# Gated delta rule in a diffusion trunk kernel: beta folded into the block inverses, 64-column products in place of masked 128-column ones, element work redistributed over four engines, and a final norm by tiles

## The chip, the cores and the metric

One core of a Trainium2 chip runs the whole program as one launch. The metric is the device time in microseconds; smaller is better. All arithmetic named here is float32.

## The reference

The reference is one inference step of a two-layer trunk over 1152 tokens (1024 of a sample, 128 of a prompt) with width 1024. Two parts of it matter.

The first is the gated DeltaNet of layer 1, which runs over each sequence forwards and backwards, with 8 heads of 64. For a chunk with keys K, queries Q, values V, gates beta and summed log-decays gc, let gamma[i,j] = exp(gc[i] - gc[j]) for j <= i. It solves A U = beta V and A W = beta exp(gc) K, with A = I + strict(beta K K^T gamma); then, with a state S that goes from chunk to chunk,

```python
v_new = u_i - w_i @ S
o = (q * exp(gc)) @ S + (tril(q @ k.T) * gamma) @ v_new
S = S * exp(g_last) + (k * exp(g_last - gc)).T @ v_new
```

The second is the final RMSNorm: y = x * rsqrt(mean(x*x) + eps) * gain, for each token.

## The kernel before

The program is a row of stages with a barrier between any two. The stages of the delta rule are `delta_prepare` (gdnp), `delta_blocks` (gdna), `delta_chunks` (gdnc) and `delta_outputs` (gdno); `final_norm` comes last.

The kernel uses chunks of 128 tokens: 9 tiles, 2 directions, 18 items (`items`). `delta_blocks` writes K K^T and Q K^T of each tile to DRAM and inverts the 16 x 16 diagonal blocks of A on VectorE; its M is first scaled by beta, with one instruction for each half of the partitions (L2243).

`delta_chunks` handles three items at a time in a software pipeline: iteration n prepares item n+1, inverts item n and carries the state through item n-1. The inverse T is built from its 16-blocks in three levels (32, 64, 128). A level computes, for each head, W = part^T T, then T W, and subtracts it. `part` is the decayed K K^T masked by GpSimd to the blocks that this level joins (L2537, `joins`); beta is a factor with which ScalarE takes W out of PSUM (L2415). Levels 1 and 2 also transpose T on TensorE (L2384), and ScalarE copies that to TT (L2419). VectorE subtracts (L2513, and on TT in the last level L2515). A level's products are written in two groups of four heads, `hg`, with one PSUM bank each for a and b.

The state part (`scan`) has four steps: step 0 multiplies K and Q by S (L2347) and VectorE forms r = beta V - beta exp(gc) K S (L2465, L2469) and mq (L2466); step 1 is T r (L2354), copied to vn (L2474); step 2 is AT vn (L2359), added up in mq and o (L2481, L2486, L2488); step 3 is kd^T vn (L2363), by which VectorE updates S in eight instructions (L2495). Steps 1 and 2 take 128 columns for a head, of which 64 are used.

The preparation: E is the row of gc broadcast to all partitions by a DMA (L2313); VectorE subtracts (L2433), ScalarE takes abs (L2423) and exp (L2428), which gives `gam`. VectorE multiplies kg (L2444) and AT (L2457) by gam, writes T's blocks by the mask `own` (L2447) and makes egk and egl, 8 numbers a partition (L2452, L2454). GpSimd masks AT (L2541), makes the three parts, TT's blocks (L2549), vb = beta V (L2555) and kd (L2562).

Every engine's order is written out by hand and kept by semaphores; TensorE interleaves level li's first products, scan step li, then level li's second products. SyncE issues each item's loads in order and waits before each for its buffer. In `final_norm` SyncE loads 9 tiles of x and then the gain. ScalarE squares and sums each tile and takes a root for groups of 4, 4 and 1 tiles (L235, L239). VectorE scales all tiles of a group (L253), multiplies each by the gain (L1925), and SyncE stores it (L1910).

## Time and profile before

| | us |
|---|---|
| median of 3 runs (lowest, highest) | 4721.29 (4719.97, 4725.55) |
| the profiled execution's own time | 4717.61 |
| its span | 4715.8 |
| delta_chunks: first load issued to the state's last update | 3112.0 to 3591.1 |
| final_norm: first load issued to the end of the span | 4680.1 to 4715.8 |

Times in the rows are microseconds from the start of the span, "mean" is in ns. A float32 product shows as two records of PE (and two weight loads, PEld), a transpose as one. L lines are those of the kernel before. "xN" counts the records merged into a row; in brackets stand the idle time ahead of it and what ended it.

### The profile page before, as it was taken

To read this page: it belongs to the slowest core of one execution; us is meant where nothing else is said; L and a number is where in the kernel's file an instruction comes from. 1 tells how busy PE (TensorE), PEld (TensorE's weight loads), DVE (VectorE), ACT (ScalarE), POOL (GpSimd) and SP (SyncE) were. 2 spreads that over 40 slices of the span, in tenths; PEclk is the share of its full clock that TensorE was granted. 3 is DMA by queue.
4 is the path that set the end of the run, shared out by engine and by line. 5 is a ranking of instruction groups with operands and counts; after the bars stand their busy time and mean duration, and the time that the engine had idled before them with its cause. 6 is when DMAs were issued, how large, how long until landed. Compare 5 with 4: busy or idle time off the path is not lost. (4 is left out here: it accounts for less than half of the span.)

```text
span 4715.8 us, 62439 instructions
## 1 busy us (share of the span) xinstructions
PE 3943.4 (84%) x25842; PEld 3420.0 (73%) x25842; DVE 1757.2 (37%) x3337; ACT 866.7 (18%) x2008; POOL 683.1 (14%) x521
## 2 busy tenths in 40 slices
PE   4979978986769999996999597438886859999995
PEld 3976623444569999995999475338885659999995
DVE  3245541224531211123123454677876441121112
ACT  2113320001100110012111123424443100011001
POOL 2000110111100011002000000036651101001100
PEclk7988979997889999997999798768997979999998
DMA  4226412314547777773421402332223547777774
GB/s 151 89 82 233 148 67 98 137 40 149 201 148 268 261 266 264 268 257 117 116 89 67 108 8 76 102 88 60 73 65 130 190 154 264 268 259 267 266 268 155
DMA packets 353335, 744.94 MB, mean 158 GB/s; under 512 B 87432, under 2 KB 193559, under 8 KB 351976
## 3 DMA queue, kind: packets, MB, share of 16 engines
q1 hardware_dynamic: 333066, 683.15, 40.9%
q0 software_dynamic: 17392, 57.58, 4.5%
q8 instruction: 205, 3.36, 0.3%
q10 hardware_dynamic: 2618, 0.40, 0.1%
q14 instruction: 54, 0.44, 0.0%
HBM read 635.63 MB, written 106.10 MB: 157 GB/s over the span
## 5 line engine op out<-in xcount | busy, mean ns | idle before, releaser
L1826 PE MATMUL moe_b<-moe_xT,ffn_w 128*128 128x144 f32 x8192 | 1022.9, 287 | 0.0
L1826 PEld LDWEIGHTS moe_b<-moe_xT,ffn_w 128*128 128x128 f32 x8192 | 1012.7, 191 | 1.8
L1826 PE MATMUL moe_b<-moe_gu,ffn_w 128*128 128x144 f32 x4096 | 550.7, 288 | 0.0
L1826 PEld LDWEIGHTS moe_b<-moe_gu,ffn_w 128*128 128x128 f32 x4096 | 516.3, 190 | 4.8
L1871 DVE TENSOR_TENSOR moe_gu<-moe_sg,moe_b 128x144 f32<-128x144 f32 x256 | 77.9, 304 | 782.3 <-PE moe_b L1826 782.3
L1851 ACT ACTIVATE moe_yT<-moe_b 128x144 f32<-128x144 f32 x256 | 74.6, 291 | 1074.8 <-PE moe_b L1826 1074.8
L2380 PE MATMUL gdnc_a<-gdnc_T,gdnc_part 128*128 128x128 f32 x864 | 139.3, 318 | 156.7 <-POOL gdnc_part L2537 88.0
L1859 DVE TENSOR_SCALAR moe_xT<-moe_x,keep_coef 128x128 f32<-128x128 f32 (+1 forms) x544 | 154.7, 346 | 252.2 <-PE moe_x L1778 252.1
L2380 PEld LDWEIGHTS gdnc_a<-gdnc_T,gdnc_part 128*128 128x128 f32 x864 | 128.0, 229 | 162.7 <-POOL gdnc_part L2537 149.9
L1747 POOL DMA_INDIRECT scratch_x<-moe_ys,moe_slot x32 | 51.8, 1619 | 1260.7 <-DVE moe_yp L1881 1260.7
L297 PE MATMUL proj_mm<-proj_hT_low,proj_w_high 128*128 128x384 f32 x576 | 193.2, 335 | 0.0
L297 PE MATMUL proj_mm<-proj_hT_high,proj_w_low 128*128 128x384 f32 x576 | 193.1, 335 | 0.0
L297 PE MATMUL proj_mm<-proj_hT_high,proj_w_high 128*128 128x384 f32 x576 | 193.1, 335 | 0.0
L1878 DVE SCALAR_TENSOR_TENSOR moe_ys<-moe_y,keep_gate_s,moe_rowg 128x512 f32<-128x512 f32 x64 | 48.1, 751 | 352.0 <-PE moe_y L1790 352.0
L297 PE MATMUL proj_mm<-proj_w_high,proj_hT_low 128*128 128x416 f32 (+1 forms) x504 | 176.1, 350 | 0.0
L297 PE MATMUL proj_mm<-proj_w_high,proj_hT_high 128*128 128x416 f32 (+1 forms) x504 | 175.7, 349 | 0.0
L297 PE MATMUL proj_mm<-proj_w_low,proj_hT_high 128*128 128x416 f32 (+1 forms) x504 | 174.7, 347 | 0.0
L2415 ACT ACTIVATE gdnc_W<-gdnc_a,gdn_beta 128x128 f32<-128x128 f32 x432 | 121.9, 379 | 229.6 <-PE gdnc_a L2380 229.6
L978 ACT ACTIVATE attnrun_prob<-attn_sc_sb,attnrun_neg 128x513 f32<-128x513 f32 (+5 forms) x144 | 107.4, 746 | 278.7 <-DVE attnrun_neg L949 277.2
L1848 ACT ACTIVATE moe_sg<-moe_b 128x144 f32<-128x144 f32 x256 | 74.5, 291 | 456.2 <-PE moe_b L1826 456.2
L2537 POOL TENSOR_TENSOR gdnc_part<-gdnc_kg,gdn_joins 128x1024 f32<-128x1024 f32 x54 | 143.5, 2671 | 94.7 <-DVE gdnc_kg L2444 94.7
L900 DVE COPY attnrun_pT<-attnrun_pt 128x512 f32<-128x512 f32 (+4 forms) x144 | 103.9, 721 | 141.9 <-PE attnrun_pt L840 141.7
(413 smaller groups left out, 6401.2 us busy)
## 6 DMA issues: line engine op xcount, KB each, us to landing
ffn_w<-moe_w_gate SPq DMA_DIRECT2D x32, 4096.0 KB, 15.8
ffn_w<-moe_w_up SPq DMA_DIRECT2D x32, 4096.0 KB, 13.9
ffn_w<-moe_w_down SPq DMA_DIRECT2D x32, 4096.0 KB, 15.7
attnrun_m_w<-w_ada SPq DMA_DIRECT2D x40, 1024.0 KB, 9.4
scratch_conv<-proj_zf POOLq DMA_DIRECT2D x24, 512.0 KB, 3.0
scratch_tm<-proj_tm SPq DMA_DIRECT2D x45, 208.0 KB, 1.9
proj_w_raw<-even_w_in SPq DMA_DIRECT2D x24, 384.0 KB, 4.2
scratch_spec<-filt_res SPq DMA_DIRECT2D x36, 256.0 KB, 2.1
```

Of the source, the lines that this page charges most:

```text
L297: mm = nc.tensor.matmul(out, lhs(a, k), rhs(b, k), start=n == 0, stop=n == len(passes) - 1)
L900: nc.vector.tensor_copy(pT[:, u % 2, 0:n], slot(("p", u))[:, 0:n]).then_inc(pT_done, 1)
L978: nc.scalar.activation(prob[:, u % 2, at:end], sc_sb[:, u % SB, at:end], ACT.Exp, bias=neg[:, u % 4:u % 4 + 1], accum_out=rs[:, g % 2, h:h ...
L1747: nc.gpsimd.indirect_dma_start(out=io["x"][l], out_offset=bass.IndirectOffsetOnAxis(ap=sl[par][:, 0:1], axis=0), in_=src[par][:], in_offse ...
L1826: mm = nc.tensor.matmul(bk[(m * FC + f) % 3][:, 0:SLOTS], w[m][:, k, f * P:(f + 1) * P], src[:, k, :], start=k == 0, stop=k == KD - 1)
L1848: nc.scalar.activation(sg[:, f, :], bk[f % 3][:, 0:SLOTS], ACT.Silu).then_inc(sg_done, 1)
L1851: nc.scalar.activation(yT[:, f, :], bk[(2 * FC + f) % 3][:, 0:SLOTS], ACT.Copy).then_inc(yT_done, 1)
L1859: ins = nc.vector.tensor_scalar(xT[:, k, cols], bx[k % 2][:, cols], co[:, 0, k:k + 1], co[:, 1, k:k + 1], ALU.mult, ALU.add)
L1871: nc.vector.tensor_tensor(gu[:, f, :], sg[:, f, :], bk[(FC + f) % 3][:, 0:SLOTS], ALU.mult).then_inc(gu_done, 1)
L2380: mm = nc.tensor.matmul(ba[hg][:, h, :], part[(n * LEVELS + li) % (LEVELS + 1)][:, 4 * hg + h, :], Tm[b][:, 4 * hg + h, :], start=True, st ...
L2415: ins = nc.scalar.activation(W[:, h, :], ba[hg][:, h % 4, :], ACT.Copy, scale=beta[:, t, d, h:h + 1])
L2537: nc.gpsimd.tensor_tensor(part[k % (LEVELS + 1)][:], kg[i][:], joins[:, li, d, :].unsqueeze(1).broadcast_to(HW), ALU.mult).then_inc(part_d ...
```

## The change

It does the following.

- beta goes into the 16-block inverses: the diagonal of Y starts as beta instead of 1, and M is scaled along its rows in both directions in one instruction. T is then A^-1 times beta, W needs no factor, r becomes V - exp(gc) K S, and begc, vb and the factor at W go away.
- The level products move only the 64 columns of T that a level reads and write 64; the mask `joins` is applied by VectorE as it takes W from PSUM. In the last level W (64 columns) is the stationary operand. Scan steps 1 and 2 move 64 columns for a head. PSUM has separate banks for K S, Q S, T r and the state.
- GpSimd masks gam and multiplies kg and AT by it, makes egk and egl, kd, TT's blocks, and the addition to o where o was written before. ScalarE forms |gc_i - gc_j| with a bias, one instruction for a head, and T's blocks with 8 copies scaled by `own`; it starts two items ahead.
- gam, kd and mq get two buffers, kg and TT three. TensorE's order becomes: first products of level 0, step 0, second products of level 0, first of 1, step 1, second of 1, first of 2, steps 2 and 3, second of 2.
- `final_norm` loads the gain behind the first tile, takes one root a tile, and scales and multiplies in one VectorE instruction.

Its core, with unchanged and lesser lines left out:

```diff
-            load_x(sp, io, x, x_in, {"x": io["x"][1]})
-            sp.dma_start(gain[:], all_rows(io["norm_final"])).then_inc(gain_in, 16)
+            for t in range(NT):
+                load_x(sp, io, x, x_in, {"x": io["x"][1]}, t)
+                if t == 0:
+                    sp.dma_start(gain[:], all_rows(io["norm_final"])).then_inc(gain_in, 16)
...
         def _(act):
-            norm.scalar(act, lambda eng, t: eng.wait_ge(x_in[t], 16))
...
+            for t in range(NT):
+                act.wait_ge(x_in[t], 16)
+                if t:
+                    act.wait_ge(squared, t)
+                nc.scalar.activation(sq[:], x[:, t, :], ACT.Square, accum_out=ss[:, t:t + 1]).then_inc(squared, 1)
+                act.wait_ge(squared, t + 1)
+                nc.scalar.activation(rstd[:, t:t + 1], ss[:, t:t + 1], ACT.Sqrt, bias=eps[:], scale=1.0 / D).then_inc(rooted, 1)
...
-            norm.vector_eps()
+            nc.vector.memset(eps[:], EPS).then_inc(eps_set, 1)
             dve.wait_ge(gain_in, 16)
+            for t in range(NT):
+                dve.wait_ge(rooted, t + 1)
+                nc.vector.reciprocal(rstd[:, t:t + 1], rstd[:, t:t + 1]).then_inc(recip, 1)
+                dve.wait_ge(recip, t + 1)
+                nc.vector.scalar_tensor_tensor(x[:, t, :], x[:, t, :], rstd[:, t:t + 1], gain[:], ALU.mult, ALU.mult).then_inc(y_done, 1)
...
-            dve.wait_ge(gate_act, 6)
-            nc.vector.tensor_tensor(begc[:], egc[:], beta[:], ALU.mult)
...
-            nc.gpsimd.memset(Y[:].rearrange("p t i c -> p t (i c)")[:, :, 0:BASE * BASE:BASE + 1], 1.0).then_inc(Y_set, 1)
+            pool.wait_ge(bb_in, 16)
+            nc.gpsimd.tensor_copy(Y[:].rearrange("p t i c -> p t (i c)")[:, :, 0:BASE * BASE:BASE + 1], bb[:]).then_inc(Y_set, 1)
...
-                scale = bb[at].unsqueeze(3 - d).broadcast_to([half, NT, BASE, BASE])
-                nc.vector.tensor_tensor(M[at], M[at], scale, ALU.mult).then_inc(M_step, 1)
...
+            nc.vector.tensor_tensor(M[:], M[:], bb[:].unsqueeze(3).broadcast_to([P, NT, BASE, BASE]), ALU.mult).then_inc(M_step, 1)
...
+        gam = [s.sb(f"gam{i}", HW) for i in range(2)]
+        kg = [s.sb(f"kg{i}", HW) for i in range(3)]
...
-        part = [s.sb(f"part{i}", HW) for i in range(LEVELS + 1)]
         Tm = [s.sb(f"T{i}", HW) for i in range(2)]
...
+        TT = [s.sb(f"TT{i}", HW) for i in range(3)]
+        W = s.sb("W", [P, HEADS, HALF])
...
+        ba = [s.ps(f"a{i}", [P, BANK]) for i in range(2)]
...
+        bz = s.ps("z", [P, BANK])
+        bs = s.ps("s", [P, BANK])
+        bk = s.ps("k", [P, BANK])
+        bq = s.ps("q", [P, BANK])
...
+        quad = lambda a: a[:, 0:4 * HALF].rearrange("p (h c) -> p h c", c=HALF)
...
+        def earlier(a, li, d):
+            return a.rearrange("p (x s c) -> p x s c", s=2, c=BASE << li)[:, :, d, :]
...
-                    sp.wait_ge(part_done, LEVELS * (p - 1))
-                sp.dma_start(kg[i][:], io["kk"][t]).then_inc(kk_in[i], 16)
-                if p >= 2:
                     sp.wait_ge(T_set, p - 1)
                     sp.wait_ge(TT_set, p - 1)
                 for w in range(2):
                     sp.dma_start(Tc[i][:, w], io["inv"][w, (2 * t + d) * HEADS:(2 * t + d + 1) * HEADS].rearrange("h p c -> p h c")).then_inc(inv_in[i], 16)
+                if p >= 3:
+                    sp.wait_ge(W_mm, lvl(p - 3, LAST, 1))
+                sp.dma_start(kg[p % 3][:], io["kk"][t]).then_inc(kk_in[p % 3], 16)
...
+                for bank, src in ((bk, KT), (bq, QT)):
...
+                        mm = nc.tensor.matmul(bank[:, j * P:(j + 1) * P], src[:, j, at], S[:, st, j, :], start=True, stop=True)
...
-                if q:
-                    pe.wait_ge(S_done, q)
...
+                    mm = nc.tensor.matmul(bz[:, h * HD:(h + 1) * HD], TT[q % 3][:, h, :], r[:, h * HD:(h + 1) * HD], start=True, stop=True)
...
+                    mm = nc.tensor.matmul(bk[:, h * HD:(h + 1) * HD], AT[q % 3][:, h, :], vn[:, h * HD:(h + 1) * HD], start=True, stop=True)
             else:
+                if q:
+                    pe.wait_ge(S_done, q)
...
+                    mm = nc.tensor.matmul(bs[:, j * P:(j + 1) * P], kd[q % 2][:, j * P:(j + 1) * P], vn[:, j * P:(j + 1) * P], start=True, stop=True)
...
+        def level_w(pe, n, li):
...
+            if li == 0:
+                pe.wait_ge(kg_done, n + 1)
+                pe.wait_ge(T_set, n + 1)
+            for hg in range(2):
+                if n or li:
+                    pe.wait_ge(TU_done, lvl(n, li - 1, hg))
+                for h in range(4):
+                    mm = nc.tensor.matmul(quad(ba[hg])[:, h, :], kg[n % 3][:, 4 * hg + h, :], earlier(Tm[n % 2][:, 4 * hg + h, :], li, d), start=True, stop=True)
+                mm.then_inc(W_mm, 1)
+                if li:
+                    for h in range(4):
+                        mm = nc.tensor.transpose(bb[hg][:, h, :], Tm[n % 2][:, 4 * hg + h, :], keep.ident[:])
+                    mm.then_inc(T_turned, 1)
+        def level_u(pe, n, li):
...
+            rows, cols = slice(HALF * d, HALF * d + HALF), slice(HALF * (1 - d), HALF * (1 - d) + HALF)
+            if li == 0:
+                pe.wait_ge(TT_set, n + 1)
+            for hg in range(2):
+                pe.wait_ge(W_taken, lvl(n, li, hg))
+                if li:
+                    pe.wait_ge(TT_done, tt(n, li, hg))
+                for h in range(4):
+                    if li < LAST:
+                        mm = nc.tensor.matmul(quad(ba[hg])[:, h, :], TT[n % 3][:, 4 * hg + h, :], W[:, 4 * hg + h, :], start=True, stop=True)
+                    else:
+                        mm = nc.tensor.matmul(quad(ba[hg])[rows, h, :], W[:, 4 * hg + h, :], TT[n % 3][:, 4 * hg + h, cols], start=True, stop=True)
+                mm.then_inc(TU_mm, 1)
...
+                q = n - 1
+                if n < N_IT:
+                    level_w(pe, n, 0)
+                scan(pe, q, 0)
+                if n < N_IT:
+                    level_u(pe, n, 0)
+                    level_w(pe, n, 1)
+                scan(pe, q, 1)
+                if n < N_IT:
+                    level_u(pe, n, 1)
+                    level_w(pe, n, 2)
+                scan(pe, q, 2)
+                scan(pe, q, 3)
+                if n < N_IT:
+                    level_u(pe, n, 2)
...
+            def set_blocks(p, half):
+                if half == 0:
+                    act.wait_ge(inv_in[p % 2], 32 * (p // 2 + 1))
+                    if p >= 2:
+                        act.wait_ge(T_turned, tt(p - 2, LAST, 1))
+                for b in range(half * NB // 2, (half + 1) * NB // 2):
+                    ins = nc.scalar.activation(Tm[p % 2][:, :, b * BASE:(b + 1) * BASE], Tc[p % 2][:, 0], ACT.Copy, scale=own[:, b:b + 1])
+                if half:
+                    ins.then_inc(T_set, 1)
+            def take_turned(n, li):
+                for hg in range(2):
+                    act.wait_ge(T_turned, tt(n, li, hg))
+                    nc.scalar.activation(TT[n % 3][:, 4 * hg:4 * hg + 4, :], bb[hg][:], ACT.Copy).then_inc(TT_done, 1)
+            for n in range(-2, N_IT):
+                p, e = n + 1, n + 2
+                if e < N_IT:
...
+                    act.wait_ge(gc_in[e % 2], 16 * (e // 2 + 1))
+                    for h in range(HEADS):
+                        ins = nc.scalar.activation(E_[e % 2][:, h, :], E_[e % 2][:, h, :], ACT.Abs, bias=gc[:, t, d, h:h + 1], scale=-1.0)
...
+                if 0 <= p < N_IT:
+                    set_blocks(p, 0)
+                if n >= 0:
+                    take_turned(n, 1)
+                if 0 <= p < N_IT:
+                    set_blocks(p, 1)
+                if n >= 0:
+                    take_turned(n, 2)
+                if e < N_IT:
+                    act.wait_ge(abs_done, e + 1)
+                    if e >= 2:
+                        act.wait_ge(AT_done, e - 1)
+                        act.wait_ge(egk_done, e - 1)
+                    nc.scalar.activation(gam[e % 2][:], E_[e % 2][:], ACT.Exp, scale=-1.0).then_inc(gam_done, 1)
+        def take_w(dve, n, li):
...
+            for hg in range(2):
+                dve.wait_ge(W_mm, lvl(n, li, hg))
+                nc.vector.tensor_tensor(W[:, 4 * hg:4 * hg + 4, :], quad(ba[hg]), joins[:, li, d, :].unsqueeze(1).broadcast_to([P, 4, HALF]), ALU.mult).then_inc(W_taken, 1)
+        def take_u(dve, n, li):
...
+            rows, cols = slice(HALF * d, HALF * d + HALF), slice(HALF * (1 - d), HALF * (1 - d) + HALF)
+            for hg in range(2):
+                dve.wait_ge(TU_mm, lvl(n, li, hg))
+                if li < LAST:
+                    dst = earlier(Tm[n % 2][:, 4 * hg:4 * hg + 4, :].rearrange("p h i -> p (h i)"), li, d)
+                    nc.vector.tensor_tensor(dst, dst, ba[hg][:, 0:4 * HALF].rearrange("p (x c) -> p x c", c=BASE << li), ALU.subtract).then_inc(TU_done, 1)
                 else:
+                    dst = TT[n % 3][rows, 4 * hg:4 * hg + 4, cols]
+                    nc.vector.tensor_tensor(dst, dst, quad(ba[hg])[rows], ALU.subtract).then_inc(TU_done, 1)
...
+            for n in range(N_IT + 1):
+                live, q = n < N_IT, n - 1
+                if live:
+                    take_w(dve, n, 0)
+                    take_u(dve, n, 0)
                 if q >= 0:
+                    t, d, st = items[q]
+                    dve.wait_ge(x_mm, 4 * q + 1)
+                    nc.vector.tensor_tensor(heads(r[:]), heads(bk[:]), spread(egc[:, t, d, :]), ALU.mult).then_inc(r_step, 1)
+                    if q >= 2:
+                        dve.wait_ge(o_added, sum(not f for f in first[:q - 1]))
+                    nc.vector.tensor_tensor(heads(mq[q % 2][:]), heads(bq[:]), spread(egc[:, t, d, :]), ALU.mult).then_inc(mq_done, 1)
+                    dve.wait_ge(r_step, q + 1)
+                    nc.vector.tensor_tensor(r[:], kv[:, t, 1, :], r[:], ALU.subtract).then_inc(r_done, 1)
+                if live:
+                    take_w(dve, n, 1)
+                    take_u(dve, n, 1)
+                if q >= 0:
+                    dve.wait_ge(x_mm, 4 * q + 2)
+                    nc.vector.tensor_copy(vn[:], bz[:]).then_inc(vn_done, 1)
+                if live:
+                    take_w(dve, n, 2)
+                if q >= 0:
+                    dve.wait_ge(x_mm, 4 * q + 3)
+                    dve.wait_ge(mq_done, q + 1)
+                    dst = o[:, t, :] if first[q] else mq[q % 2][:]
+                    nc.vector.tensor_tensor(dst, mq[q % 2][:], bk[:], ALU.add).then_inc(o_step, 1)
+                if live:
+                    take_u(dve, n, 2)
+                if q >= 0:
+                    dve.wait_ge(egl_done, q + 1)
+                    dve.wait_ge(x_mm, 4 * q + 4)
+                    for h in range(HEADS):
...
+                        ins = nc.vector.scalar_tensor_tensor(S[rows, st, j, rows], S[rows, st, j, rows], egl[rows, q % 3, h:h + 1],
+                                                             bs[rows, j * P + rows.start:j * P + rows.stop], ALU.mult, ALU.add)
+                    ins.then_inc(S_done, 1)
...
+            for n in range(-1, N_IT + 2):
+                p, q = n + 1, n - 2
                 if p < N_IT:
...
+                    g = gam[p % 2]
+                    pool.wait_ge(gam_done, p + 1)
+                    nc.gpsimd.tensor_tensor(g[:], g[:], incl[:, d, :].unsqueeze(1).broadcast_to(HW), ALU.mult).then_inc(gam_masked, 1)
+                    pool.wait_ge(gam_masked, p + 1)
+                    pool.wait_ge(kk_in[p % 3], 16 * (p // 3 + 1))
+                    nc.gpsimd.tensor_tensor(kg[p % 3][:], kg[p % 3][:], g[:], ALU.mult).then_inc(kg_done, 1)
+                    pool.wait_ge(inv_in[p % 2], 32 * (p // 2 + 1))
+                    if p >= 3:
+                        pool.wait_ge(x_mm, 4 * (p - 3) + 2)
...
+                    nc.gpsimd.tensor_tensor(TT[p % 3][:].rearrange("p h (b c) -> p h b c", c=BASE),
+                                            Tc[p % 2][:, 1].unsqueeze(2).broadcast_to([P, HEADS, NB, BASE]), own_mask, ALU.mult).then_inc(TT_set, 1)
                     pool.wait_ge(qk_in[p % 3], 16 * (p // 3 + 1))
+                    nc.gpsimd.tensor_tensor(AT[p % 3][:], AT[p % 3][:], g[:], ALU.mult).then_inc(AT_done, 1)
+                    last = P - 1 if d == 0 else 0
+                    nc.gpsimd.tensor_copy(egk[:, p % 3, :], g[:, :, last]).then_inc(egk_done, 1)
+                    pool.wait_ge(egk_done, p + 1)
+                    if p >= 3:
+                        pool.wait_ge(S_done, p - 2)
+                    nc.gpsimd.tensor_tensor(egl[:, p % 3, :], egk[:, p % 3, :], egc[:, t, d, :], ALU.mult).then_inc(egl_done, 1)
+                if 0 <= n < N_IT:
+                    if n >= 2:
+                        pool.wait_ge(x_mm, 4 * (n - 1))
+                    nc.gpsimd.tensor_tensor(heads(kd[n % 2][:]), heads(kv[:, t, 0, :]), spread(egk[:, n % 3, :]), ALU.mult).then_inc(kd_done, 1)
+                if q >= 0 and not first[q]:
...
+                    pool.wait_ge(o_step, q + 1)
+                    nc.gpsimd.tensor_tensor(o[:, t, :], o[:, t, :], mq[q % 2][:], ALU.add).then_inc(o_added, 1)
```

## Rows read from the trace of the kernel before

**Rows 1.** The page's first part: busy time, share of the span, instructions

```profile
PE 3943.4 (84%) x25842; PEld 3420.0 (73%) x25842; DVE 1757.2 (37%) x3337; ACT 866.7 (18%) x2008; POOL 683.1 (14%) x521
```

**Rows 2.** Busy time by stretch, delta_chunks; last columns: granted clock, DMA share, GB/s

```profile
3308.00:3334.00 26.00, 22.12 (x179) 21.81 (x180) 20.52 (x31) 11.86 (x33) 15.34 (x7) 0.93 0.23 67
...
3542.00:3568.00 26.00, 23.53 (x182) 23.28 (x183) 15.36 (x28) 8.96 (x30) 10.02 (x6) 0.87 0.01 1
...
3318.00:3320.00 2.00, 2.00 (x12) 2.00 (x12) 2.00 (x4) 0.54 (x3) 2.00 (x2) 0.57 0.00 0
```

**Rows 3.** Timeline of a middle item: start, length, engine, line, what

```profile
3311.47 5.57 POOL L2537 TENSOR_TENSOR gdnc_part<-gdnc_kg,gdn_joins 128x1024 f32<-128x1024 f32 x2 [5.75 <-DVE gdnc_kg L2444]
...
3312.45 2.32 DVE L2452 COPY gdnc_egk<-gdnc_gam 128x8 f32<-128x8 f32 x1
...
3314.80 2.26 DVE L2454 TENSOR_TENSOR gdnc_egl<-gdnc_egk,gdn_egc 128x8 f32<-128x8 f32 x1
...
3317.81 1.62 PE L2380 MATMUL gdnc_a<-gdnc_T,gdnc_part 128*128 128x128 f32 x8 [3.33 <-DVE gdnc_T L2513]
```

**Rows 4.** Timeline of the first item's start and of the last item inverted

```profile
3126.22 3.78 PE L2380 MATMUL gdnc_a<-gdnc_T,gdnc_part 128*128 128x128 f32 x16 [88.00 <-POOL gdnc_part L2537]
...
3554.51 1.95 PE L2380 MATMUL gdnc_a<-gdnc_T,gdnc_part 128*128 128x128 f32 x16
...
3555.61 2.18 ACT L2415 ACTIVATE gdnc_W<-gdnc_a,gdn_beta 128x128 f32<-128x128 f32 x8 [4.86 <-PE gdnc_a L2380]
...
3558.09 1.95 PE L2396 MATMUL gdnc_b<-gdnc_W,gdnc_TT 128*128 128x128 f32 x16
3559.18 0.69 DVE L2513 TENSOR_TENSOR gdnc_T<-gdnc_T,gdnc_b 128x512 f32<-128x512 f32 x1 [0.46 <-PE gdnc_b L2396]
3559.99 0.97 PEld L2380 LDWEIGHTS gdnc_a<-gdnc_T,gdnc_part 128*128 128x128 f32 x8
...
3560.98 0.60 PE L2384 MATMUL gdnc_b<-keep_ident,gdnc_T 128*128 128x128 f32 x4
...
3574.47 1.13 PE L2347 MATMUL gdnc_x<-gdn_S,gdn_KT 128*128 128x128 f32 x8 [0.64 <-DVE gdnc_mq L2481]
```

**Rows 5.** Groups by line in delta_chunks: count, busy us, mean ns of one

```profile
L2541 POOL TENSOR_TENSOR gdnc_AT<-gdnc_AT,gdn_incl 128x1024 f32<-128x1024 f32 x18 | 46.3, 2573 | 114.7 <-DMA gdnc_AT<-scratch_qk 114.5
...
L2562 POOL TENSOR_TENSOR gdnc_kd<-gdn_kv,gdnc_egk 128x512 f32<-128x512 f32 x18 | 18.8, 1042 | 74.7 <-PE gdnc_z L2363 74.7
...
L2481 DVE TENSOR_TENSOR gdnc_mq<-gdnc_mq,gdnc_x 128x256 f32<-128x256 f32 x34 | 12.7, 414 | 0.0
...
L2469 DVE TENSOR_TENSOR gdnc_r<-gdnc_vb,gdnc_r 128x512 f32<-128x512 f32 x18 | 12.3, 682 | 0.0
...
L2495 DVE SCALAR_TENSOR_TENSOR gdn_S<-gdn_S,gdnc_egl,gdnc_z 64x64 f32<-64x64 f32 x136 | 38.1, 280 | 2.3
```

**Rows 6.** Weight loads (128 columns) of products that move 64 and 72 columns

```profile
1104.69 1.78 PEld L1380 LDWEIGHTS hyena_b<-hyena_bwd_p,hyena_Y 128*128 128x128 f32 x8 [5.58 <-POOL hyena_Y L1447]
...
2976.76 0.53 PEld L2021 LDWEIGHTS gdnp_bg<-gdn_g,gdn_incl 128*128 128x128 f32 x4
```

**Rows 7.** Busy time by stretch in other stages; columns as in rows 2

```profile
1104.60:1110.00 5.40, 4.20 (x16) 3.64 (x16) 3.50 (x13) 1.26 (x4) 0.04 (x1) 0.50 0.08 24
...
2960.00:2980.00 20.00, 8.05 (x64) 6.96 (x64) 12.98 (x17) 9.06 (x17) 0.00 (x0) 1.00 0.00 0
...
4692.00:4694.00 2.00, 0.00 (x0) 0.00 (x0) 0.00 (x0) 1.82 (x5) 0.00 (x0) 0.50 1.01 404
```

**Rows 8.** delta_blocks' scaling, and final_norm's loads, bytes and gain products

```profile
3060.29 5.14 DVE L2243 TENSOR_TENSOR gdna_M<-gdna_M,gdna_bb 64x2304 f32<-64x2304 f32 x2
...
4680.09 4.29 SPq L285 DMA_DIRECT2D final_x<-scratch_x  x9
...
DMA packets 2736, 9.96 MB, mean 249 GB/s; under 512 B 304, under 2 KB 304, under 8 KB 2736
...
4698.10 4.62 DVE L1925 TENSOR_TENSOR final_x<-final_x,final_gain 128x1024 f32<-128x1024 f32 x4
```

253 lines of the change are left out of this document (37 added, 216 removed).

## The prediction, made before the changed kernel was run

> **What bounds the kernel now.** I read the page's shares first: TensorE is busy 84% of the span, but over stages with other limits [rows 1], so the changed stages have to be read by themselves. delta_chunks comes next, by stretches: in 26 us PE is busy 22.1, VectorE 20.5, GpSimd 15.3 and ScalarE 11.9, and the granted clock averages 0.93 [rows 2]. No engine is full, so I took the timeline of one item. At 3317.81 the first products of level 1 start after 3.33 us idle, behind VectorE's T. VectorE was held by two instructions on 8 numbers each, 2.32 and 2.26 us, and both lie inside GpSimd's 5.57 us of two mask products [rows 3]: VectorE waited for GpSimd. After the idle time the clock stands at its lower level, 1.2 GHz, for part of the next stretch, with an average of 0.57 while PE has work [rows 2]. So the bound is TensorE's stream of products plus that stall and what it does to the clock.
>
> Two periods measure it. From the first product of item 0 (3126.22) to that of item 17 (3554.51) is 428.3 us for 17 items, 25.19 each. Item 17, with nothing prepared beside it, takes 3554.51 to 3574.47 = 19.96 [rows 4]. The stall, other waits and the clock thus cost 5.2 us an item.
>
> **The price of a 64-column product.** This decides how far PE's stream shrinks. Records of 128 columns: 16 in 1.95 us with the last one 0.275 long, so (1.95-0.275)/15 = 0.112 apart; two records a product give 0.223, and 8 products 1.79 [rows 4]. A transpose: (0.60-0.275)/3 = 0.108, so 4 take 0.43 [rows 4]. Products that move 64 columns with 128 columns of weights show weight loads (1.78-0.333)/7 = 0.207 apart (0.333 is the length of one) with the clock at 0.50 [rows 6, 7], which would be 0.103 at 1.00. With 72 columns at 1.00 they are (0.53-0.19)/3 = 0.113 apart [rows 6, 7]. The weight load sets the pace, and fewer moved columns hardly help. I take 0.107: a product 0.214, 8 products 1.71, a saving of 4%. Bounds: 0.223 as now, and half of it, 0.112, if only moved columns counted. The Trainium skill has a rule for each end ("TensorE: Matmul & The Clock Gate"): "LDWEIGHTS (loading the stationary operand)" gives P/1.2 ns for P weight columns, 107 ns for 128, while "Back-to-back issue gap" gives N/2.4 + 2.5 ns, 29 ns for each of four passes at N = 64. The rows side with the first, and show besides that the load doubles at the lower clock.
>
> Only the last level's second products have 64 weight columns. I estimate half, 0.43 for four, with 0.86 as the upper bound.
>
> **The new iteration, by TensorE's order.** First products of level 0: 1.71; step 0: 8 of 128 columns, 1.79; second products of level 0: 1.71; first of level 1 with 8 transposes: 1.71+0.86 = 2.57; step 1: 1.71; second of 1: 1.71; first of 2 with transposes: 2.57; step 2: 1.71; step 3: 4 of 128 columns, 0.89. The last level's second products take 0.43 for the first four, and then the next item's first products must wait for VectorE. From the last record's start that is 0.275 to its end, 0.03 to VectorE, 0.41 for 256 columns (L2481), 0.12 to the weight load, 0.84 [rows 4, 5]. The second four lie inside it. Sum: 17.6.
>
> Between levels 0 and 1, and 1 and 2, the same 0.84 is hidden by the other four products (0.86). At level 0 VectorE first updates S: from the end of the last level 0.3+0.4, then 8 x 0.28 = 2.3 and the first W 0.4, 3.5; TensorE arrives after 1.27-0.43+1.71+1.79 = about 4, so nothing. At step 1, VectorE's T is done 0.72 after the last second product of level 0 started, then come r, mq and the subtraction, 0.6+0.6+0.68 [rows 5], and 0.12: 2.7 against 2.57+0.1. I charge 0.1: **17.7**.
>
> **What moves to GpSimd.** Three products of 1024 at 2.57, TT's blocks about 2, kd 1.04, the addition to o 1.3 in 10 of 18 items, two tiny ones: 12 us an item [rows 5], under 17.7. VectorE loses E, kg, AT, T's blocks, egk, egl and the copy or addition of o; it keeps 12 instructions of 256 columns (5.0), five of 512 (3.4) and S (2.3), 10.7 against 20. ScalarE: 16 of 128 elements at 2.18/8 = 0.27 [rows 4], four copies of 0.6 and an exp of 1.1, 7.8. All have cover while TensorE streams.
>
> What stays exposed is the subtraction for r, the one large VectorE instruction left with both inputs in SBUF. In the old order it was never held (GpSimd waited for VectorE then), so no row prices it: nothing at the low end (the change's GpSimd chain, begun at exp, about 2 us before an item's start, has done gam, kg, TT and AT by about 7, where the subtraction starts), one whole product, 2.4, at the high end. The nearest rows are the holds of egk and egl [rows 3], but those always met the middle of a product; here only AT's end and the small kd (1.04) are near. I take 0.5. The Trainium skill ("SBUF — State Buffer", "SBUF: two separate sides") says a VectorE instruction with two SBUF inputs is fully blocked until GpSimd's is over; by that alone it would pay the full remainder, up to the high end.
>
> Period: **18.2**. Seventeen of them save 17 x (25.19-18.2) = 118.8. Item 17 saves 19.96-17.7 = 2.3.
>
> **Rest of delta_chunks.** SyncE's loads are the same 1.7 MB an item. kg's load moves behind the two of the blocks and behind a wait for level 2's first products of three items before, which are long done by then; E goes out two items ahead behind step 2 and lands before ScalarE's products are needed. The start: kg needs abs (8 x 0.27), exp and two GpSimd products, but no VectorE work and no mask product, about 2 us less than now. The tail (3574.47 to 3591.1) has one vn copy for two, 64-column steps, and o's addition beside S: 1.0 less. Bounds for both together: 0 and 5.
>
> **Other stages.** delta_blocks: two scalings of 5.14 together become one, -2.6 [rows 8]. delta_prepare: a VectorE product of 144 numbers, -0.3. GpSimd's copy of beta lies under VectorE's work.
>
> final_norm: now VectorE starts only after the gain, and needs 4.62/4 = 1.16 a tile for the gain on top of the scale [rows 8]. After, one such instruction and a small reciprocal do for a tile, and ScalarE adds a small root; I estimate 1.5 a tile for either, begun some 6 us after the first load, so that VectorE would end near 4700. But the loads and stores are 9.96 MB [rows 8] and DMA runs full at 404 GB/s [rows 7]: 24.7 us from about 4681.5, to 4706.5. The stores queue behind the loads. The span ended at 4715.8: **-9** (bounds -5, if stores start late, and -13, if DMA is no limit).
>
> **Sum.** 118.8+2.3+2+1.0+2.6+0.3+9 = 136.0. Against the profiled execution's 4717.61 that is 4581.6; the median of the runs is 3.7 above that execution, so 4585.3. I say **4586**.
>
> **Rivals.**
> A (8%): moved columns count, not weights. 56 products fall by about 0.1 each, 5.6; but four products (0.45) no longer hide 0.84, which puts back about 0.4 at two places and 0.5 before step 1. Period 14.0: 17.7 x 4.2 = 74 less, **4512**. Against it stand both weight-load rows.
> B (18%): GpSimd holds the subtraction in full at each item, 1.9 more, and ScalarE's row of small instructions is late by a few tenths; period 20.3, **4622**. For it: VectorE was held in full in every item of the old order. Against: GpSimd has 6 us of slack an item.
> C (3%), slower: half-width moves leave the granted clock at 1.2 GHz. The PE content of 17.2 doubles, the period is about 35, and 17 items lose 10 each: near **4880**. It turns slower than before once the lower clock holds for some 8 us of added time an item. Against it: transposes alone, with PE busy 8 of 20 us, kept 1.00 [rows 7]; for it: 1.2 GHz in the 64-column stretch, though that followed idle time.
> D (2%): a late load or a GpSimd product of two full operands near 4 us makes the preparation the bound, period 23: 4668.
> The forecast's own case has 69%: 4560 to 4612, from the bounds of 4% on products, 0 to 1.2 for the hold, and final_norm.
>
> **How the numbers follow.** The range 4550 to 4630 takes in the forecast's case and most of B, and leaves out A, C and D with a little of both, 2 in 10. Of no change within 0.2% (about what a measurement of this kernel can tell) I see almost none: only between D and C. Faster 0.96, same 0.01, slower 0.03.
>
> **What would show it.** Right: level products' weight loads 0.10 to 0.11 apart at full clock; the last level's under 0.07; period 18 to 18.5; clock near 1.00 across delta_chunks; no VectorE instruction above 1 us but the subtraction at times; PE's longest wait per item under 1 us; final_norm with DMA at 400 GB/s until the end, span from its first load 26 to 27 us. Wrong: weight loads 0.06 apart (A), the subtraction at 2 to 3 us (B), a clock of 0.5 while PE is busy (C), TensorE waiting for GpSimd's kg or TT (D).

## The result, and the profile after

The changed kernel takes **4597.89 us** (median of 4 runs, 4595.32 to 4598.86) against 4720.63 for the kernel before on the same chip (4 runs): ratio 0.9737, 95% interval 0.972 to 0.9754. The forecast was 4586 with a range of 4550 to 4630. So the sign, the size and the likeliest case held, and the gain is 12 us smaller than said. The profiled execution took 4598.86 us with a span of 4597.1, 118.7 less than the span before.

The loop first. A middle item by the timeline of the changed kernel (start, length, engine, line, what), TensorE's groups and the two engines that meet at r:

```profile
3297.63 1.97 PE L2377 MATMUL gdnc_a<-gdnc_T,gdnc_kg 128*128 128x64 f32 x16
3297.83 2.34 POOL L2528 TENSOR_TENSOR gdnc_kg<-gdnc_kg,gdnc_gam 128x1024 f32<-128x1024 f32 x1
...
3301.28 1.90 PE L2395 MATMUL gdnc_a<-gdnc_W,gdnc_TT 128*128 128x64 f32 x16
...
3302.02 2.36 POOL L2536 TENSOR_TENSOR gdnc_AT<-gdnc_AT,gdnc_gam 128x1024 f32<-128x1024 f32 x1
...
3304.32 0.19 POOL L2538 COPY gdnc_egk<-gdnc_gam 128x8 f32<-128x8 f32 x1
...
3304.60 0.20 POOL L2542 TENSOR_TENSOR gdnc_egl<-gdnc_egk,gdn_egc 128x8 f32<-128x8 f32 x1
3304.75 0.68 DVE L2492 TENSOR_TENSOR gdnc_r<-gdn_kv,gdnc_r 128x512 f32<-128x512 f32 x1
3304.76 1.57 POOL L2548 TENSOR_TENSOR gdnc_kd<-gdn_kv,gdnc_egk 128x512 f32<-128x512 f32 x1
...
3305.63 1.90 PE L2354 MATMUL gdnc_z<-gdnc_r,gdnc_TT 128*128 128x64 f32 x16
...
3314.54 1.01 PEld L2397 LDWEIGHTS gdnc_a<-gdnc_TT,gdnc_W 128*64 128x64 f32 x16
3314.54 1.15 PE L2397 MATMUL gdnc_a<-gdnc_TT,gdnc_W 128*64 128x64 f32 x16
```

The next item's first product starts at 3315.83: the period is **18.20**, as forecast, against 25.19. egk and egl take 0.19 and 0.20 us on GpSimd where VectorE took 2.32 and 2.26 [rows 3], and the stall of 3.33 us is gone. Windows of the changed kernel (stretch, length, busy time of PE, PEld, DVE, ACT, POOL, granted clock, DMA share, GB/s), a middle item and the first two:

```profile
3302.00:3320.00 18.00, 17.86 (x169) 17.63 (x168) 10.05 (x25) 7.70 (x21) 10.58 (x8) 1.00 0.34 89
3125.80:3148.00 22.20, 22.19 (x112) 21.78 (x112) 4.65 (x11) 9.14 (x24) 11.88 (x11) 0.50 0.39 106
3148.00:3170.30 22.30, 22.16 (x170) 21.91 (x169) 8.00 (x18) 7.77 (x21) 12.36 (x8) 0.81 0.06 15
```

In the middle TensorE is busy 17.86 of 18.00 us at a clock of 1.00 (before: 22.1 of 26 at 0.93 [rows 2]); VectorE has fallen from 20.5 us of 26 to 10 of 18. But the first two items take 22.22 and 22.25: PE is busy all the time, at 0.50, its lower level of 1.2 GHz. All fifteen later periods are 18.2.

The start, by the timeline of the changed kernel:

```profile
3110.32 0.33 SPq L2317 DMA_DIRECT2D gdnc_E<-scratch_gcT  x1
...
3116.91 1.06 ACT L2457 ACTIVATE gdnc_gam<-gdnc_E 128x1024 f32<-128x1024 f32 x1
...
3120.46 2.35 POOL L2528 TENSOR_TENSOR gdnc_kg<-gdnc_kg,gdnc_gam 128x1024 f32<-128x1024 f32 x1
...
3120.88 2.44 ACT L2442 ACTIVATE gdnc_E<-gdnc_E,gdn_gc 128x128 f32<-128x128 f32 x8 [2.92 <-DMA gdnc_E<-scratch_gcT]
...
3123.23 2.43 ACT L2427 ACTIVATE gdnc_T<-gdnc_Tc,gdn_own 128x128 f32<-128x128 f32 x8
...
3125.81 1.51 PE L2377 MATMUL gdnc_a<-gdnc_T,gdnc_kg 128*128 128x64 f32 x6 [86.76 <-ACT gdnc_T L2427]
```

kg is ready at 3122.81, but the first product starts at 3125.81, behind ScalarE's T blocks. Those stand in ScalarE's order behind abs of the second item, for whose E ScalarE sat idle for 2.92 us. From first load to first product it is 15.49 us, where it was 14.18 before (3112.04 to 3126.22 [rows 4]).

The end, by windows of final_norm (columns as above), from the first load at 4568.80 to the end of the span at 4597.1:

```profile
4570.00:4574.00 4.00, 0.00 (x0) 0.00 (x0) 0.00 (x0) 1.61 (x3) 0.00 (x0) 0.50 0.94 288
4574.00:4580.00 6.00, 0.00 (x0) 0.00 (x0) 4.04 (x6) 5.18 (x12) 0.00 (x0) 0.50 1.02 417
...
4586.00:4592.00 6.00, 0.00 (x0) 0.00 (x0) 2.55 (x3) 0.89 (x3) 0.00 (x0) 0.50 1.03 421
```

VectorE's last product ends at 4588.6 and the last store goes out at 4588.61; DMA works off what is queued. The stage takes 28.3 us in place of 35.7.

**Where the 118.7 us are.** Loop, first product of item 0 to that of item 17: 428.29 before, 317.37 after (3125.81 to 3443.18), 110.9 less. Item 17: 18.00 for 19.96, 2.0 less. The tail, from its first scan product to the next stage's first load: 17.45 for 17.74, 0.3 less. The start: 1.3 more. final_norm: 7.4 less. All up to the loop's first load: 1.7 less. The stages between, which the change leaves alone: 2.3 more. Stages that are the same in two kernels wander by some us from one execution to the next (the loop's first load was issued at 3110.3 to 3120.4 in the executions below), so a difference of a few us is read inside its stage. For the same reason medians of two kernels compare to some 3 us: the kernel before took 4720.63 beside the changed kernel, and 4722.56 to 4723.72 beside the kernels below.

### The profile page after: what moved, and what is told of

It is laid out like the page before. It is cut to its first block and busy times, and to the rows that moved or that the text cites. A ratio compares the mean times of both kernels' runs of the same rounds, so it can differ in the third digit from the quotient of the medians.

```text
span 4597.1 us, 62121 instructions
## 1 busy us (share of the span) xinstructions
PE 3907.1 (85%) x25842; PEld 3385.4 (74%) x25842; DVE 1574.5 (34%) x3278; ACT 822.7 (18%) x1852; POOL 609.1 (13%) x530
## 5 line engine op out<-in xcount | busy, mean ns | idle before, releaser
L2377 PE MATMUL gdnc_a<-gdnc_T,gdnc_kg 128*128 128x64 f32 x864 | 116.3, 284 | 88.9 <-ACT gdnc_T L2427 86.8
L2377 PEld LDWEIGHTS gdnc_a<-gdnc_T,gdnc_kg 128*128 128x128 f32 x864 | 110.2, 202 | 90.9 <-issue 90.8
L854 PE MATMUL attnrun_po<-attn_tok,attnrun_pT 128*128 128x128 f32 x960 | 145.5, 293 | 1.0 <-DVE attnrun_o_sb L914 0.8
L832 PE MATMUL attnrun_sc<-attn_KT,attn_QT 64*128 64x384 f32 (+3 forms) x416 | 135.7, 436 | 0.0
```

The source lines that it names most:

```text
L832: mm = nc.tensor.matmul(psc[u % 2][:, lo:lo + k.shape[1]], q, k, start=True, stop=True)
L854: mm = nc.tensor.matmul(po[:, h, :], pT[:, u % 2, i * P:(i + 1) * P], v, start=i == 0, stop=i == len(tiles) - 1)
L2377: mm = nc.tensor.matmul(quad(ba[hg])[:, h, :], kg[n % 3][:, 4 * hg + h, :], earlier(Tm[n % 2][:, 4 * hg + h, :], li, d), start=True, stop= ...
```

## The experiments

Twelve kernels, on three questions and a version that opens better. One figure recurs, read from each one's timeline: the **opening**, from the loop's first load to the first product of its third item. It is 63.8 us in the kernel before (3112.04 to 3175.82) and 60.0 in the changed one (3110.32 to 3170.28), where at 18.2 an item and a start of 14 it could be 50. Line numbers in rows are those of the kernel shown, a few more where lines were added.

### Why is the clock low in the first two items?

**warm512.** Products ahead of the loop; otherwise the changed kernel:

```diff
         def _(pe):
+            for k in range(10):
+                nc.tensor.matmul(bq[:], keep.ident[:], KT[:, 0, 0:MIX], start=True, stop=True)
             for n in range(N_IT + 1):
```

> The changed kernel with ten products of 512 columns on TensorE ahead of the first item, in the time in which it waits for its operands; their sums go to a bank that is overwritten later. In the changed kernel the first two periods of the delta rule loop take 22.2 us each, at granted clocks of 0.50 and 0.81, and every later one 18.2. Theory (the clock is low there because TensorE stood still before the first item, and the first item's stream of 64-column products does not raise it): the ten products raise the clock before the first item and it stays up; the first two periods fall to 18 us each, and about 8 us go, unless the first product is held up. Rival 1 (the 64-column stream of an item without scan steps cannot hold the high clock either): the clock falls back during the first item and the gain is under 3 us. Rival 2 (the low clock there has to do with the start of the stage and not with what TensorE does): no change, both periods at 22.2.

**warm64.** Against warm512:

```diff
-            for k in range(10):
-                nc.tensor.matmul(bq[:], keep.ident[:], KT[:, 0, 0:MIX], start=True, stop=True)
+            for k in range(60):
+                nc.tensor.matmul(bq[:, 0:HALF], keep.ident[:], KT[:, 0, 0:HALF], start=True, stop=True)
```

> The same as warm512, but with sixty products of 64 columns in place of ten of 512: about the same busy time of TensorE (at the low clock 60 by 0.21 us = 12.6 us). Theory (64-column products with 128 weight columns keep TensorE's records busy and do not raise the clock): the clock stays at 0.50 through them, and the first two periods stay near 22 us. Rival (any busy stream of that length raises it): the first period falls to about 18 us as with wide products.

Windows of warm512 and then of warm64:

```profile
3112.00:3115.00 3.00, 3.00 (x5) 1.25 (x4) 0.00 (x0) 0.01 (x1) 0.00 (x0) 0.50 1.02 215
3115.00:3118.00 3.00, 3.00 (x8) 1.29 (x8) 0.00 (x0) 2.97 (x9) 0.00 (x0) 0.98 0.86 251
...
3122.00:3125.80 3.80, 0.00 (x0) 0.00 (x0) 0.00 (x0) 3.80 (x14) 3.80 (x3) 0.94 0.95 361
3125.80:3127.00 1.20, 1.14 (x6) 1.17 (x6) 0.00 (x0) 0.87 (x1) 1.20 (x1) 0.50 0.23 63
```

```profile
3125.00:3130.00 5.00, 5.00 (x25) 5.00 (x25) 0.00 (x0) 4.46 (x14) 4.66 (x4) 0.50 0.81 202
...
3148.00:3154.00 6.00, 6.00 (x31) 6.00 (x30) 1.27 (x3) 1.77 (x6) 0.00 (x0) 0.50 0.23 26
```

The 512-column products raised the clock at once, so it isn't the stage. They ended 3.9 us too early: TensorE stood idle, the clock was back at 0.50, and the first two periods were 22.2 and 22.0. In warm64 the sixty products took 25.8 us and not 12.6 (a product is two records of 0.21, which my expectation forgot), held the first item up by 10 us, and the clock stayed at 0.50 through them and the first item, from 3110 to 3158, with PE busy without a gap. The theory's part on 64-column products holds; the forecast gain failed. Medians: 4599.55 and 4611.33 (ratios 0.9738 and 0.9764 to the kernel before).

**warm14.** Against warm512:

```diff
-            for k in range(10):
+            for k in range(14):
```

> As warm512, with fourteen products of 512 columns in place of ten. In warm512 they ran from 3111.21, the clock rose to 1.00 by 3115, the ten ended at 3121.97, TensorE then stood for 3.89 us and the first item ran at 0.50. Four more at 0.86 us each end at about 3125.4, 0.4 us before the first product (3125.8 in the changed kernel). Theory (a busy stream of the loop's own products holds a clock that is already high, and cannot raise one that is low): the first item runs at 1.00, both first periods come near 18 us or less, the first nearer 12 (64-column products at 0.11 us a record), and some 10 us go. Rival (the first item's products of 64 columns cannot hold it either): the clock falls within the first item, and less than 4 us go.

Windows of warm14, then its timeline in the second item:

```profile
3129.00:3141.00 12.00, 11.76 (x109) 11.46 (x110) 4.64 (x11) 8.49 (x22) 11.76 (x10) 1.00 0.65 164
...
3153.00:3161.00 8.00, 8.00 (x42) 8.00 (x42) 2.29 (x5) 0.60 (x1) 0.00 (x0) 0.52 0.00 0
```

```profile
3148.22 2.36 POOL L2538 TENSOR_TENSOR gdnc_AT<-gdnc_AT,gdnc_gam 128x1024 f32<-128x1024 f32 x1
...
3148.43 2.69 DVE L2494 TENSOR_TENSOR gdnc_r<-gdn_kv,gdnc_r 128x512 f32<-128x512 f32 x1
...
3151.17 2.00 PE L2354 MATMUL gdnc_z<-gdnc_r,gdnc_TT 128*128 128x64 f32 x16 [1.70 <-DVE gdnc_r L2494]
```

Both answers at once. The first item's own stream keeps a clock that is already high: 12.2 us at 1.00. But GpSimd is now behind TensorE, its AT runs when the subtraction for r is issued, the subtraction takes 2.69 us for 0.68, TensorE stands 1.70 us, and in the 64-column stream behind that the clock is 0.52: the second period is 26.7 us. The opening fell by 6.0 (to 53.96), not by 10, and the median (4599.78) doesn't show it.

**wide.** The level products move 128 columns again:

```diff
-mm = nc.tensor.matmul(quad(ba[hg])[:, h, :], kg[n % 3][:, 4 * hg + h, :], earlier(Tm[n % 2][:, 4 * hg + h, :], li, d), start=True, stop=True)
+mm = nc.tensor.matmul(ba[hg][:, h * P:(h + 1) * P], kg[n % 3][:, 4 * hg + h, :], Tm[n % 2][:, 4 * hg + h, :], start=True, stop=True)
...
-mm = nc.tensor.matmul(quad(ba[hg])[:, h, :], TT[n % 3][:, 4 * hg + h, :], W[:, 4 * hg + h, :], start=True, stop=True)
+mm = nc.tensor.matmul(ba[hg][:, h * P:(h + 1) * P], TT[n % 3][:, 4 * hg + h, :], W[:, 4 * hg + h - h % 2:4 * hg + h - h % 2 + 2, :], start=True, stop=True)
```

> The changed kernel with the level products of the delta rule loop moving 128 columns in place of 64 (the product with kg at all three levels, the second product at the first two), as before the change; what the other engines read is as in the changed kernel, so the values are not those of the reference. Theory (a pair of 128 weight columns and 64 moved columns costs what 128 and 128 cost, because the weight load of 0.11 us sets the pace): the steady period stays at 18.2 us, within 0.2, and at the start the clock rises some microseconds after the first product, as in the kernel before (0.50 until 3130, 1.00 from 3132), so that the first periods take less: 5 to 9 us go in all, and the kernel with double the columns is faster than the changed one. Rival (the moved columns count): the period grows by 80 records at 0.05 us, 4 us, and the loop by 70 us.

Windows of wide, whose first product starts at 3130.79, then its timeline in the middle:

```profile
3134.00:3138.00 4.00, 4.00 (x26) 4.00 (x26) 1.27 (x3) 1.53 (x6) 3.92 (x3) 0.65 0.85 339
3138.00:3142.00 4.00, 4.00 (x38) 3.95 (x37) 1.27 (x3) 2.36 (x6) 3.92 (x5) 1.00 0.01 4
...
3157.50:3160.50 3.00, 3.00 (x16) 3.00 (x16) 0.21 (x1) 0.00 (x0) 0.00 (x0) 0.50 0.00 0
```

```profile
3309.35 1.04 POOL L2548 TENSOR_TENSOR gdnc_kd<-gdn_kv,gdnc_egk 128x512 f32<-128x512 f32 x1
3309.37 1.57 DVE L2492 TENSOR_TENSOR gdnc_r<-gdn_kv,gdnc_r 128x512 f32<-128x512 f32 x1
...
3311.00 2.00 PE L2354 MATMUL gdnc_z<-gdnc_r,gdnc_TT 128*128 128x64 f32 x16 [0.54 <-DVE gdnc_r L2492]
```

At the start the theory holds: with 128 columns and no other change of place, the clock is at 1.00 some 6 us after the first product, and the opening is 51.9, 8.1 less than with 64. That opening holds warm14's stall too: in the second item the subtraction for r takes 2.65 us and TensorE stands for 1.62, and the clock falls, but here it is back after 3 us (3157.5 to 3160.5) where warm14's 64-column stream stayed low for 13.5 (3153.5 to 3167.0). In the middle both were off: the period is 19.17, 0.97 more, neither 0 nor 4. Of that 0.54 is a wait for r, and the groups of products are 0.4 longer, for 40 products of twice the columns: 0.01 us each. The median is 4609.66: 15 longer periods outweigh the shorter opening.

### Who holds whom?

**egk_dve.** egk and egl back on VectorE:

```diff
                 if live:
                     take_w(dve, n, 0)
+                    if n + 1 < N_IT:
+                        decays(n + 1)
                     take_u(dve, n, 0)
```

(`decays` is the copy and the product of the kernel before, behind a wait for gam's mask; GpSimd's two instructions go.)

> The changed kernel with the two small operations for the decays (egk and egl, 128x8 each, 0.2 us each on GpSimd) back on VectorE, between the first level's masking and its subtraction; the rest as in the changed kernel. Theory (they are held under GpSimd's products and that hold is what stopped TensorE for 3.3 us an item before): they take 1 to 2.3 us each again, the subtraction behind them is late by 2 us or more, and the period grows from 18.2 to between 20 and 22 us, 35 to 65 us over the loop. Rival (most of the gain came from the smaller work of all engines, and VectorE now has enough slack to hide the hold): the period grows by less than 0.5 us, under 9 us over the loop.

Timeline of egk_dve, the start, a middle item and the next:

```profile
3125.57 0.17 DVE L2485 COPY gdnc_egk<-gdnc_gam 128x8 f32<-128x8 f32 x1 [23.21 <-POOL gdnc_gam L2538]
...
3125.77 2.21 DVE L2487 TENSOR_TENSOR gdnc_egl<-gdnc_egk,gdn_egc 128x8 f32<-128x8 f32 x1
...
3275.73 2.35 POOL L2549 TENSOR_TENSOR gdnc_AT<-gdnc_AT,gdnc_gam 128x1024 f32<-128x1024 f32 x1
3275.83 2.27 DVE L2487 TENSOR_TENSOR gdnc_egl<-gdnc_egk,gdn_egc 128x8 f32<-128x8 f32 x1
...
3278.49 1.10 PE L2377 MATMUL gdnc_a<-gdnc_T,gdnc_kg 128*128 128x64 f32 x8 [1.60 <-DVE gdnc_T L2472]
...
3298.49 1.97 PE L2377 MATMUL gdnc_a<-gdnc_T,gdnc_kg 128*128 128x64 f32 x8 [1.61 <-DVE gdnc_T L2472]
...
3303.56 3.51 PE L2354 MATMUL gdnc_z<-gdnc_r,gdnc_TT 128*128 128x64 f32 x16
```

The median is 4684.46, **87 us** more than the changed kernel (83 when each is set against the kernel before beside it; the loop itself is 83 longer in the trace), for two instructions on 8 numbers a partition: more than the theory's 65. That the length is a hold, and not VectorE's own time for them, the first item shows: its egk began 0.04 us before GpSimd's product and took 0.17, and egl behind it, inside that product, 2.21. In the middle the hold gives 1.6 us of wait an item and a period of 20.0 (3251.32 to 3271.34). But in seven of the sixteen items behind the first the clock falls at that wait (the later row of L2377 takes 1.97 us for what took 1.10) and stays low for 13.5 to 24 us: such an item takes 26.5 to 30.9, here 28.1 (3291.34 to 3319.41). The hold itself is some 2 us an item, about 30 in all; the rest, nearly twice that, is its effect on the clock.

**b_egk_pool.** The reverse, in the kernel before: the two instructions go from VectorE to GpSimd, behind TT, and nothing else changes.

```diff
-                nc.vector.tensor_copy(egk[:, p % 3, :], gam[:, :, last]).then_inc(egk_done, 1)
-                dve.wait_ge(egk_done, p + 1)
-                nc.vector.tensor_tensor(egl[:, p % 3, :], egk[:, p % 3, :], egc[:, t, d, :], ALU.mult).then_inc(egl_done, 1)
...
+                    nc.gpsimd.tensor_copy(egk[:, p % 3, :], gam[:, :, last]).then_inc(egk_done, 1)
+                    pool.wait_ge(egk_done, p + 1)
+                    nc.gpsimd.tensor_tensor(egl[:, p % 3, :], egk[:, p % 3, :], egc[:, t, d, :], ALU.mult).then_inc(egl_done, 1)
```

> The kernel before with the two small operations for the decays (egk and egl, 128x8) on GpSimd, behind its product TT, in place of VectorE; all else as before. Theory (they are held under GpSimd's products on VectorE and cost some 2.2 us each, and that is what makes TensorE wait for VectorE's T, 3.33 us in the middle of each item): they take 0.2 us each on GpSimd; VectorE has 4.6 us less an item; the wait of 3.33 us goes, and the period falls from 25.2 to about 22 us, as far as the clock stays up, 50 to 60 us in all, so that about half of the whole gain needs no other part of the change. Rival (another wait takes its place: GpSimd's own order is then 0.4 us later for the masks that TensorE waits for, or VectorE's other operations are held in their place): the period falls by less than 1 us, under 20 us in all.

Median 4656.6, 66 us less than the kernel before (ratio 0.9863, 0.9848 to 0.9878): **more than half of the whole gain**. The window of one of its items, and a stretch of another:

```profile
3302.80:3323.90 21.10, 19.17 (x168) 18.86 (x169) 17.43 (x27) 10.48 (x31) 15.62 (x9) 1.00 0.30 82
...
3240.50:3244.00 3.50, 3.50 (x19) 3.50 (x18) 3.12 (x4) 2.85 (x10) 1.44 (x1) 0.53 0.00 0
```

The period is 21.1, not 25.2 (the theory said 22). TensorE still waits some 1.9 to 2.3 us an item for VectorE's T, and yet the clock of this item is 1.00. In four of the items behind the first it does fall at that wait (the second row), but with products of 128 columns behind the wait it is back after 3.5 us, and such an item takes 22.8 to 23.1. So a fall makes its item some 1.7 us longer here and 7 to 11 in egk_dve. What is left to the changed kernel's 18.2 is 2.9 us an item: 1.8 are TensorE's idle time (1.93 us in this window, 0.14 in the changed kernel's), 0.8 the last level's products (1.15 us for 1.95, with 64 weight columns). No run takes these two apart.

**at_last.** GpSimd makes AT behind kd instead of ahead of egk:

```diff
-                    pool.wait_ge(qk_in[p % 3], 16 * (p // 3 + 1))
-                    nc.gpsimd.tensor_tensor(AT[p % 3][:], AT[p % 3][:], g[:], ALU.mult).then_inc(AT_done, 1)
                     last = P - 1 if d == 0 else 0
...
                     nc.gpsimd.tensor_tensor(heads(kd[n % 2][:]), heads(kv[:, t, 0, :]), spread(egk[:, n % 3, :]), ALU.mult).then_inc(kd_done, 1)
+                if p < N_IT:
+                    pool.wait_ge(qk_in[p % 3], 16 * (p // 3 + 1))
+                    nc.gpsimd.tensor_tensor(AT[p % 3][:], AT[p % 3][:], gam[p % 2][:], ALU.mult).then_inc(AT_done, 1)
```

> The changed kernel with one move in GpSimd's order: the masking product AT (2.36 us) comes behind kd instead of ahead of the two small operations for the decays. In the changed kernel VectorE's subtraction for r begins 0.01 us before GpSimd's kd and is not held; kd is (1.57 us instead of 1.04). Theory (of two such operations whose operands all lie in SBUF, the one that starts second is held until the other ends): kd now runs some 2.3 us earlier, AT runs from about 3303.6 to 3306.0 in the middle period that begins at 3297.6, the subtraction is held under it for about 1.2 us, step 1 of the scan waits for r, and the period grows from 18.2 to about 19.2 us, 15 us and more over the loop. Rival (the two engines only slow each other a little, and the long 2.3 us of the small operations before was something else): the period stays within 0.2 us of 18.2.

Timeline of at_last:

```profile
3312.74 2.37 POOL L2549 TENSOR_TENSOR gdnc_AT<-gdnc_AT,gdnc_gam 128x1024 f32<-128x1024 f32 x1
3314.05 1.61 DVE L2492 TENSOR_TENSOR gdnc_r<-gdn_kv,gdnc_r 128x512 f32<-128x512 f32 x1
...
3315.71 2.00 PE L2354 MATMUL gdnc_z<-gdnc_r,gdnc_TT 128*128 128x64 f32 x16 [0.62 <-DVE gdnc_r L2492]
```

AT ends at 3315.11 and the subtraction 0.55 later: it waited for AT and then ran. Period 19.07 (3306.93 to 3326.01), median 4613.97, 16 us more than the changed kernel (13 when each is set against the kernel before beside it). In the trace the loop is 8.7 us longer: 15 periods by 0.87, less 4.6 in the first two, because the clock rose at 3153.5, 20 us after the first product, and not some 30 us after it as in the changed kernel; why, no run shows. This is the forecast's rival B made on purpose, at 0.9 us an item; which engine is held is a matter of order. In the changed kernel VectorE begins 0.01 us ahead of kd and kd takes 1.57; in wide kd begins 0.02 ahead and the subtraction takes 1.57. The rows for r and mq, whose input is a PSUM bank, stay at 0.68 in all of them. The Trainium skill ("SBUF — State Buffer", "SBUF: two separate sides") says that the one which starts first gets the shared ports for the whole instruction and the other fully blocks; these rows agree, in both directions.

### What is the pace of TensorE's stream?

**narrow.** The products with kg get 64 weight columns in place of 128 (from the second item on, half of each result left out):

```diff
-mm = nc.tensor.matmul(quad(ba[hg])[:, h, :], kg[n % 3][:, 4 * hg + h, :], earlier(Tm[n % 2][:, 4 * hg + h, :], li, d), start=True, stop=True)
+mm = nc.tensor.matmul(quad(ba[hg])[0:HALF, h, :], kg[n % 3][:, 4 * hg + h, 0:HALF], earlier(Tm[n % 2][:, 4 * hg + h, :], li, d), start=True, stop=True)
```

> The changed kernel with the weights of the 48 records of the products with kg cut from 128 to 64 columns (from the second item on; half of each result is left out, so the values are not those of the reference). Theory (weight columns set the pace; the last level's product, which has 64 of them and 64 moved, takes 0.061 us a record against 0.112): the three parts lose 48 by 0.05 = 2.4 us; the first shorter one lets TensorE reach the scan's step 1 before VectorE's r is done, which gives back up to 1 us; period 15.8 to 16.8 us, 24 to 41 us less over the loop. Rival (the pace is set by something that all products share, such as their number): the period stays at 18.2.

Timeline of narrow, levels 0 and 1:

```profile
3318.95 1.12 PE L2380 MATMUL gdnc_a<-gdnc_T,gdnc_kg 128*64 128x64 f32 x16
...
3322.24 1.97 PE L2398 MATMUL gdnc_a<-gdnc_W,gdnc_TT 128*128 128x64 f32 x16 [0.20 <-DVE gdnc_W L2466]
...
3324.14 0.68 PE L2380 MATMUL gdnc_a<-gdnc_T,gdnc_kg 128*64 128x64 f32 x8
...
3324.75 0.66 PE L2384 MATMUL gdnc_b<-keep_ident,gdnc_T 128*128 128x128 f32 x4
```

The level-0 group falls from 1.81 to 1.05 us (16 records, 0.065 each for 0.113): weight columns set the pace, moved columns don't. But the period falls only to 17.6, by 0.6 and not by 1.4 to 2.4. The groups at levels 1 and 2, four products and four transposes in turn, fall by 0.24 and 0.32 in place of 0.8, as a transpose group of 128 weight columns behind a short one is longer (0.66 for 0.61, and its successor later). Step 0 and the next group lose 0.6, of which 0.20 is a wait for VectorE's W. The median, 4595.33, can't tell this from the changed kernel, and the trace says why: the 15 shorter periods give 8.4 us, but the second item takes 26.3 us for 22.3, because its subtraction for r is held under AT (2.74 us), TensorE stands for 1.98, and the clock is at 0.50 for the 17 us behind that (3162.5 to 3179.5). So "a product costs its weight load" is right inside a run of equal products, and I was wrong to carry it to mixed ones.

**b_final.** The kernel before with the changed final_norm alone (the same edit as in the diff of the change).

> The kernel before with the changed final norm alone. Theory (the parts add up): the last stage goes from 35.7 us to 28.3 as in the changed kernel, all else as before, 7.4 us less in all, about 4713 us. Rival (part of the gain came from what precedes it in the changed kernel): under 4 us less. A difference of 7 us is 0.15% and near what the total can tell, so the stage is read from the trace.

Median 4714.26 over 10 runs, 9.1 less (ratio 0.998, 0.9971 to 0.999). Read in its trace, the stage takes 27.9 us (4686.40 to the end of the span at 4714.3), 7.8 less. The part stands by itself.

### A version that opens better

**best_cold** takes the first item's gam mask, kg and T to VectorE, which is idle there, and puts the third item's AT behind kd on GpSimd:

```diff
         @blk.vector
         def _(dve):
+            nc.vector.tensor_tensor(gam[0][:], gam[0][:], incl[:, d, :].unsqueeze(1).broadcast_to(HW), ALU.mult).then_inc(gam_masked, 1)
...
+            nc.vector.tensor_tensor(kg[0][:], kg[0][:], gam[0][:], ALU.mult).then_inc(kg_done, 1)
...
+            nc.vector.tensor_tensor(Tm[0][:].rearrange("p h (b c) -> p h b c", c=BASE),
...
-                if 0 <= p < N_IT:
+                if 0 < p < N_IT:
                     set_blocks(p, 0)
```

**best** adds warm512's loop with `range(11)`. **best2** adds one wait, so that VectorE's T isn't held under AT:

```diff
                     if p == 0:
                         pool.wait_ge(gam_masked, 1)
+                        pool.wait_ge(T_set, 1)
```

> The changed kernel with the first item's operands made in another way: its mask on gam, its kg and its T by VectorE (1.2 us each, idle there) in place of GpSimd (2.35 each) and ScalarE (4.9 behind the second item's Abs); and GpSimd makes the third item's AT behind kd. No warm-up products. Theory: the first product comes 11.5 us after the stage's first load in place of 15.5; the clock is low there, so the first two periods stay at 22.2 us each; 4 us less in all. Rival (the low clock is left earlier or later because of the shift): the first two periods change by over 2 us.

> best_cold with eleven products of 512 columns on TensorE ahead of the first item. In warm14 the warm-up let the first item run in 12.2 us at a clock of 1.00, but in the second item VectorE's subtraction for r was held under GpSimd's AT (2.69 us in place of 0.68), TensorE stood for 1.70 us, the clock fell to 0.50 in the stream of 64-column products behind it, and that period took 26.7 us. Theory (GpSimd's lead of the first items is what was missing): here it has 6 us less to do ahead of that point and AT lies behind kd, so that r is not held; first product 11.5 us after the first load, first period 12.2, second 18.2 to 19: 30.4 to 31.2 in place of 44.4 in the changed kernel, and with the 4 us of the start 17 to 18 us less than the changed kernel, about 4580 us. Rival (the clock falls again in the second item for another wait): the first two periods take 38 us or more, and the gain is 10 us or less.

> best with one wait more: GpSimd begins the first item's AT only once VectorE's T is done. In best that T was held under AT (3.38 us in place of 1.2), TensorE stood for 1.40 us between the warm-up and the first product, the clock fell from 1.00 to 0.50 two microseconds later and stayed there for the rest of the first item (first period 20.2 us). Theory (a stall of more than a microsecond ahead of a stream of 64-column products costs the clock): T takes 1.2 us and is done before the warm-up ends, the first product follows it without a gap, the first item runs at 1.00: 12.2 us, the second period 18.2 to 19, first product 12.1 us after the first load; some 9 us less than best and 14 to 16 less than the changed kernel, about 4583 us. Rival (the 64-column stream falls back by itself after some microseconds, and warm14 was an exception): the clock falls within the first item again, first period 18 us or more, no gain over best.

| | first load to first product | first two periods | opening | median of the kernel |
|---|---|---|---|---|
| changed kernel | 15.49 | 22.22, 22.25 | 60.0 | 4597.89 |
| best_cold | 13.63 | 22.23, 22.38 | 58.2 | 4597.76 |
| best | 13.50 | 20.23, 18.22 | 52.0 | 4591.63 |
| best2 | 12.63 | 17.17, 18.83 | 48.6 | 4592.59 |

best_cold won 1.9 us for the 4 expected, because T took 3.37 us under GpSimd's AT. In best the same hold left TensorE idle for 1.40 us behind the warm-up, and the clock fell: its first two periods, 38.5 us together, are those of its rival. In best2 it didn't: TensorE went on without a gap at 1.00, as expected, until it waited for ScalarE's copy of the transposed blocks. That copy stood in ScalarE's order behind abs of the third item, for whose E ScalarE had sat idle for 2.92 us, and behind four of T's blocks: the same order that made the changed kernel's start late. Timeline and windows of best2:

```profile
3133.20 1.97 PE L2395 MATMUL gdnc_a<-gdnc_W,gdnc_TT 128*128 128x64 f32 x16 [2.28 <-ACT gdnc_TT L2438]
```

```profile
3128.00:3130.00 2.00, 2.00 (x21) 2.00 (x20) 0.85 (x2) 1.05 (x4) 1.92 (x2) 1.00 0.86 147
...
3134.00:3136.00 2.00, 2.00 (x17) 2.00 (x17) 0.84 (x2) 0.70 (x3) 1.92 (x4) 0.82 0.29 93
3136.00:3140.00 4.00, 4.00 (x21) 3.67 (x21) 0.85 (x2) 0.61 (x2) 0.52 (x1) 0.50 0.30 30
```

So the expectation of 12.2 for the first period was wrong by 5 us, for a wait I hadn't looked for, and the clock paid again. The openings are 8.0 and 11.3 us shorter than the changed kernel's. best against best_cold, on one chip in one series, is 6.1 less in the medians and 6.3 in the opening. best2's runs spread from 4583 to 4600, so whether it beats best, and by how much it beats the changed kernel, its total doesn't settle; its ratio to the kernel before is 0.9723 (0.971 to 0.9736), the lowest that was measured.

## Why the prediction was right, and where it fell short

The forecast's span was 136.0 us below the profiled one and came out 118.7 below; the difference of 17.3, by its steps:

- **"17 x (25.19-18.2) = 118.8"**: 110.9. The period itself was met to 0.01, but not in the first two items, which took 22.2 each. The missing term was the clock at the loop's start (8.0). Rival C held the mechanism, that a stream of 64-column products leaves the clock low, and I gave it 3% as a case for the whole loop. It is true of a part: from a low clock, the first item ran through at 0.50, and in warm64 26 us more of such products did too. From a high clock the stream holds it. The before kernel's first item, with 128 columns, was at 1.00 from 3130.5 on, 4.3 us after its first product, where the changed kernel's took some 30.
- **The period's inside** was right by two errors that cancel. The products cost what I took, 0.107: the second products of level 0 are 16 records in 1.73 us, 0.108 each (wide's, with 128 columns, 0.112). But the ten groups of the sum took 0.56 more together: 1.81 for 1.71 at level 0, 1.04 for 0.89 at step 3, 0.02 to 0.08 at each of the others, where one kind of product follows another. And the hold of r, for which I charged 0.5, was nothing, by a lead of 0.01 us; wide and at_last show 0.5 and 0.9 us an item when the order tips. That the period came out at 18.20 and not half a microsecond off is luck.
- **The start, "about 2 us less"**: 1.3 more, a miss of 3.3. I followed kg's chain (which did end at 3122.81) and not T's, which had moved to ScalarE behind an instruction that waits for another item's load. The order of the queue that T had moved into wasn't counted.
- **The tail, 1.0**: 0.3. In both kernels the clock falls to 0.50 about a microsecond behind the wait for r there (2.82 us, and 3.41 before). In the kernel before it was back at 1.00 at 3587.9, within step 3's eight records, which took 1.52 us; in the changed kernel it stayed at 0.50, and they took 2.02. **Item 17, 2.3**: 2.0.
- **final_norm, 9**: 7.4 (7.8 in b_final). DMA is the limit, as said, at 412 to 421 GB/s; but the first tile was there only 3.6 us after its load was issued, and the stretch of 4570 to 4574 ran at 288 GB/s, which I had taken as full.
- **delta_blocks 2.6 and delta_prepare 0.3**: the removed scaling is 2.58 us by its rows (5.14 for two [rows 8], 2.56 for the one that is left). The small product in delta_prepare was worth nothing: the reciprocal behind it waits for ScalarE's table load in both kernels (2987.48 and 2987.61). Up to the loop the span is 1.7 shorter, which the wander of the executions (some us) blurs.
- The stages left alone took 2.3 us more. Sum: 7.9 + 0.3 + 3.3 + 0.7 + 1.6 + 1.2 + 2.3 = 17.3.
- Of the signs that I named for a right forecast two failed: the clock was not near 1.00 across delta_chunks, and final_norm took 28.3 us from its first load, not 26 to 27. And rival A's "17.7 x 4.2 = 74" has a wrong factor: with 17 periods it is 71, 4515. That changes no chance.

What was shown of the cause: the wait that set the period came from egk and egl on VectorE. Moving just them gives 66 of the 123 us (b_egk_pool), and moving just them back takes 83 to 87 (egk_dve). The two aren't equal, so the rest of the change and this part aren't simply additive: what a wait costs depends on the stream behind it. Of the other 57 us final_norm is 7 to 9 (b_final); most of the rest is in the loop, 360.6 us in b_egk_pool and 317.4 in the changed kernel from the first product of item 0 to that of item 17, and its parts (less work on VectorE, the last level's 64 weight columns) are argued from rows, not shown by runs. Rival A (moved columns count) is out by wide; B is real but didn't strike; D wasn't seen, GpSimd was busy 10.6 of 18 us.

Open: what ends the low clock in a 64-column stream. Behind the start or the wait that left it low, it rose after 6.5 us (best2), 13.5 to 24 (warm14, best, narrow, at_last, egk_dve), 30 to 31 (the changed kernel, warm512, best_cold) and 48 (warm64), always near the end of an item or around the next one's first products and step 0, and no run varied that alone. Open too why the same wait was followed by the low clock in some items only: 1.6 us in seven of egk_dve's, 1.9 to 2.3 in four of b_egk_pool's.

## What to carry to other kernels

Look for tiny instructions with long rows: here two of 128x8 that showed 2.3 us each were more than half of a 123 us gain, and they were found in a timeline, not in the shares. Halving the moved columns of a float32 product with 128 weight columns buys next to nothing by itself (0.4 us of an item of 18 here), and it can take away what brings the clock up again after a wait (3 to 7 us with 128 columns here, 6.5 to 30 with 64); price the start of such a loop at the lower level, and keep TensorE fed up to its first product if you warm it. When an operand's making moves to another engine, read that engine's order up to the instruction, for every operand that the first product waits for.

## What the runs showed that was not expected

- The clock. From 0.50, 512-column products raised it in 3.9 to 6.2 us (warm512, best, warm14, best2), 128-column ones in 4.3 and 6.0 (the kernel before, wide), and transposes of 128 columns alone in 3.5 (delta_prepare of the kernel before, 2949.5 to 2953.0); 64-column ones left it at 0.50 for 48 us with PE busy without a gap (warm64). At 1.00 the same stream kept it for a whole item (warm14) and for 15 items (the changed kernel). Waits of 1.2 to 2.3 us brought it down at times with either kind of product. What differs is the way back, as wide and warm14 show behind the same stall of 1.6 and 1.7 us: 3 us with 128 columns, 13.5 with 64.
- An exclusion of two engines decided by 0.01 to 0.02 us: kd is 1.57 us or 1.04 and the subtraction 0.68 or 1.57, in kernels that differ elsewhere. A period can change by 0.5 us with no change near the place.
- A run of products with 64 weight columns saves nearly half (0.065 for 0.113 a record), but far less where it alternates with groups of 128.
